# Running the last of eight experts outside the loop, and closing the trunk by token block

## What is computed

```python
h = h + moe_swiglu(hn, router_w, router_b, expert_w_gate, expert_w_up, expert_w_down)
return rms_norm(h, final_norm)      # h * rsqrt(mean(h*h) + 1e-6) * final_norm
# one expert: (silu(xb @ w_gate[e]) * (xb @ w_up[e])) @ w_down[e],  w_gate[e]: 1024 x 3584
```

## Time and profile before

| | |
|---|---|
| median of 3 runs | 1443.53 us (1442.66 to 1445.46) |
| the profiled execution | 1442.99 us, span 1441.1 us |
| TensorE matmuls busy | 1398.6 us (97%) |
| VectorE, ScalarE, GpSimd busy | 1137.7, 944.7, 20.7 us |
| granted clock, mean | 0.993 |

### The profile page before, as it was taken

The page is one execution under the profiler, slowest core; times in us unless marked ns, Lnnn a source line. Parts: engine busy times, 40 slices in busy tenths (PEclk is TensorE's granted clock), DMA queues, the critical chain, the costliest instruction groups (busy, mean ns, idle before and its releaser), DMA issues.

```text
span 1441.1 us, 17938 instructions
## 1 busy us (share of the span) xinstructions
PE 1398.6 (97%) x6483; PEld 1146.4 (80%) x6483; DVE 1137.7 (79%) x814; ACT 944.7 (66%) x773; POOL 20.7 (1%) x26
## 2 busy tenths in 40 slices
PE   6999999999979999999999999999999999999995
PEld 5888888787868887887888788788878878887884
DVE  5455666655578889888888988898898888889887
ACT  5354344445657777777777777777777777777775
POOL 0000000000120000000000000000000000000001
PEclk9999999999999999999999999999999999999998
DMA  9358775562149998998999899899989989999992
GB/s 356 106 170 225 215 207 176 175 205 88 59 135 340 371 377 304 373 369 311 367 378 355 318 370 369 315 362 365 370 307 381 363 321 372 357 353 332 368 375 85
DMA packets 192979, 423.16 MB, mean 294 GB/s; under 512 B 19184, under 2 KB 21360, under 8 KB 192944
## 3 DMA queue, kind: packets, MB, share of 16 engines
q1 hardware_dynamic: 179728, 418.15, 80.7%
q10 hardware_dynamic: 12784, 3.26, 1.6%
q0 software_dynamic: 432, 1.28, 0.3%
HBM read 421.61 MB, written 1.05 MB: 293 GB/s over the span
## 4 chain that ended last, share of the span: by engine, by line
PE 91%; DVE 3%; ACT 2%; issue 2%; POOL 0%; DMA 0%; ACTq 0%; DVEq 0%; POOLq 0%
PE bank_G L995 10%; PE bank_G L997 10%; PE bank_G L996 10%; PE bank_U L995 9%; PE bank_U L997 9%; PE bank_U L996 9%; PE bank_Y L995 8%; PE bank_Y L997 8%; PE bank_Y L996 8%; PE bank_T L1333 2%; DVE w_lo L624 1%; PE bank_G L1230 1%; PE bank_T L995 1%; PE bank_T L996 1%; PE bank_T L997 1%
## 5 line engine op out<-in xcount | busy, mean ns | idle before, releaser
L624 DVE TENSOR_TENSOR w_lo<-raw,w_hi 128x2048 fp32r<-128x2048 f32 x394 | 896.4, 2290 | 210.5 <-ACT w_hi L365 209.7
L365 ACT ACTIVATE w_hi<-raw 128x2048 fp32r<-128x2048 f32 x394 | 754.6, 1918 | 290.7 <-PE bank_U L997 93.3
L995 PE MATMUL bank_Y<-w_hi,hidT_hi 128*128 128x512 f32 x492 | 194.3, 395 | 0.0
L997 PE MATMUL bank_Y<-w_hi,hidT_lo 128*128 128x512 f32 x492 | 192.5, 391 | 0.0
L996 PE MATMUL bank_Y<-w_lo,hidT_hi 128*128 128x512 f32 x492 | 192.1, 390 | 0.0
L995 PE MATMUL bank_U<-w_hi,xg_hi 128*128 128x512 f32 x448 | 181.3, 405 | 0.5
L995 PE MATMUL bank_G<-w_hi,xg_hi 128*128 128x512 f32 x448 | 177.3, 396 | 1.4 <-DVE w_lo L624 0.5
L997 PE MATMUL bank_G<-w_hi,xg_lo 128*128 128x512 f32 x448 | 175.8, 392 | 0.0
L997 PE MATMUL bank_U<-w_hi,xg_lo 128*128 128x512 f32 x448 | 175.7, 392 | 0.0
L996 PE MATMUL bank_U<-w_lo,xg_hi 128*128 128x512 f32 x448 | 174.2, 389 | 0.0
L996 PE MATMUL bank_G<-w_lo,xg_hi 128*128 128x512 f32 x448 | 174.1, 389 | 0.0
(11 more groups left out here) (262 smaller groups left out, 1482.8 us busy)
## 6 DMA issues: line engine op xcount, KB each, us to landing
raw<-in_expert_w_gate SPq DMA_DIRECT2D x114, 1024.0 KB, 7.2
raw<-in_expert_w_up SPq DMA_DIRECT2D x113, 1024.0 KB, 7.2
raw<-in_expert_w_down SPq DMA_DIRECT2D x112, 1024.0 KB, 6.8
raw<-in_nat_w_qkv SPq DMA_DIRECT2D x12, 1024.0 KB, 5.0
raw<-in_ffn_w_gate SPq DMA_DIRECT2D x11, 1024.0 KB, 8.8
raw<-in_ffn_w_up SPq DMA_DIRECT2D x11, 1024.0 KB, 5.2
raw<-in_ffn_w_down SPq DMA_DIRECT2D x11, 1024.0 KB, 5.5
raw<-in_fourier_w_in SPq DMA_DIRECT2D x4, 1024.0 KB, 11.3
```

The costliest lines, as they stand in the source:

```text
L365: nc.scalar.activation(w_hi[w][:], raw[s][:], ACT.Copy).then_inc(hi_made, 1)
L624: nc.vector.tensor_tensor(w_lo[w][:], raw[s][:], w_hi[w][:].bitcast(f32), ALU.subtract).then_inc(lo_made, 1)
L995: nc.tensor.matmul(out_, xh, wh, start=start, stop=False)
L997: return nc.tensor.matmul(out_, xl, wh, start=False, stop=stop)
```

## The change

The loop runs over E = 0 to 6. Every engine then reads the flag and runs expert 7 once more in straight code (`expert(LAST, ...)`), with all that is for a successor left out: the three loads, the three splits, the selection, the gather with its copies, transposes and splits. The `If` follows behind it and, when taken, makes up for these. `e_scatter` counts each block and half, `e_added` each block, and `add_result` goes block by block.

The closing norm: GpSimd scales the gain row by sqrt(D) in the router stage, right behind `rstds(3)`. ScalarE squares block b as soon as its additions are done. GpSimd makes each block's factor by itself, as (sum + D eps)^-0.5. VectorE makes the output in one operation per block and half (h x factor x scaled gain), and SP stores each of the four quarters when it is made. The diff, cut:

```diff
@@ sync
+        with sp.Fori(0, LAST) as E:
+            own_loads(E)
+            next_loads(E)
         sp.wait_ge(flag_done, 1)
         over = sp.value_load(mo["flag"][0:1, 0:1], min_val=0, max_val=1)
+        own_loads(LAST)
         with sp.If(over):
...
         for b in range(NB):
-            sp.wait_ge((fin_act, fin_dve)[b], 1)
-            sp.dma_start(out[0, P * b:P * (b + 1), :], hn[:, b, :]).then_inc(s_out, 16)
+            for q in range(2):
+                sp.wait_ge(fin_done, 2 * b + q + 1)
+                cs = slice(BANK * q, BANK * (q + 1))
+                sp.dma_start(out[0, P * b:P * (b + 1), cs], hn[:, b, cs]).then_inc(s_out, 16)
@@ gpsimd
         rstds(3)
-        pool.wait_ge(moe_done, 1)
-        nc.gpsimd.tensor_tensor(hn[:, 0], h[:, 0], mo["gain"][:, 1], ALU.mult).then_inc(fin_gain, 1)
-        rstds(4)
+        nc.gpsimd.tensor_scalar(mo["gain"][:, 1], mo["gain"][:, 1], float(D) ** 0.5, None, ALU.mult).then_inc(fin_gain, 1)
+        for b in range(NB):
+            pool.wait_ge(sq_done, NB * 4 + b + 1)
+            nc.gpsimd.tensor_scalar(rstd[:, 4, b:b + 1], sumsq[:, 4, b:b + 1], D * EPS, None, ALU.add).then_inc(rstd_chain, 1)
+            pool.wait_ge(rstd_chain, 4 + 1 + b + 1)
+            nc.gpsimd.tensor_tensor(rstd[:, 4, b:b + 1], rstd[:, 4, b:b + 1], half_power[:, b:b + 1], ALU.pow).then_inc(fin_rstd, 1)
@@ scalar
             for b in range(NB):
+                if i == 4:
+                    act.wait_ge(e_added, NB * LAST + b + 1)
...
+        with act.Fori(0, LAST) as E:
+            expert(E, True)
         act.wait_ge(flag_done, 1)
         over = act.value_load(mo["flag"][0:1, 0:1], min_val=0, max_val=1)
+        expert(LAST, False)
         with act.If(over):
...
         squares(4)
-        act.wait_ge(rstd_done, 5)
-        act.wait_ge(fin_gain, 1)
-        nc.scalar.activation(hn[:, 0], hn[:, 0], ACT.Copy, scale=rstd[:, 4, 0:1]).then_inc(fin_act, 1)
@@ vector
         def add_result(E, e):
-            for q in range(2):
-                dve.wait_ge(e_scatter, 2 * E + 1 + q)
-                for b in range(NB):
+            for b in range(NB):
+                for q in range(2):
+                    dve.wait_ge(e_scatter, NB * (2 * E + q) + b + 1)
...
-            last.then_inc(e_added, 1)
+                last.then_inc(e_added, 1)
...
-        dve.wait_ge(e_added, NE)
-        dve.sem_inc(moe_done, 1)
-        dve.wait_ge(s_gain, 32)
-        link(nc.vector.tensor_tensor(hn[:, 1], h[:, 1], mo["gain"][:, 1], ALU.mult))
-        dve.wait_ge(rstd_done, 5)
-        nc.vector.tensor_scalar(hn[:, 1], hn[:, 1], rstd[:, 4, 1:2], None, ALU.mult).then_inc(fin_dve, 1)
+        dve.wait_ge(fin_gain, 1)
+        for b in range(NB):
+            dve.wait_ge(fin_rstd, b + 1)
+            for q in range(2):
+                cs = slice(BANK * q, BANK * (q + 1))
+                nc.vector.scalar_tensor_tensor(out=hn[:, b, cs], in0=h[:, b, cs], scalar=rstd[:, 4, b:b + 1],
+                                               in1=mo["gain"][:, 1, cs], op0=ALU.mult, op1=ALU.mult).then_inc(fin_done, 1)
@@ tensor
             pe.wait_ge(e_hid, E * STEPS + (STEPS - 1))
-            gather()
+            if ahead:
+                pe.wait_ge(e_sel, E + 2)
+                gather()
             down(STEPS - 2, 0)
-            transpose_tokens(E + (sweep + 2))
+            if ahead:
+                transpose_tokens(E + 2)
...
+        with pe.Fori(0, LAST) as E:
+            expert(E, True)
         pe.wait_ge(flag_done, 1)
         over = pe.value_load(mo["flag"][0:1, 0:1], min_val=0, max_val=1)
+        expert(LAST, False)
         with pe.If(over):
```

More of the change, by code:

```diff
@@ L575, in result_hi, with expert @@
                 nc.scalar.activation(mo["y_hi"][:, BANK * q:BANK * (q + 1)], Y[q][:], ACT.Copy).then_inc(e_yhi, 1)
-        def expert(E, sweep):
+        def expert(E, ahead):
             for j, (kind, c, half) in enumerate(EXPERT):
@@ L583, in expert @@
                         hidden_hi(E, c - 1)
-                if (kind, c, half) == ("up", STEPS - 1, 1):
-                    gather_copy(E + (sweep + 2))
+                if (kind, c, half) == ("up", STEPS - 1, 1) and ahead:
+                    gather_copy(E + 2)
                 if (kind, c, half) == ("down", STEPS - 2, 0):
-                    gather_hi(E + (sweep + 2))
+                    if ahead:
+                        gather_hi(E + 2)
                     hidden_hi(E, STEPS - 1)
@@ L590, in expert @@
                     result_hi(E)
-                split_hi(j + SPLIT, E)
+                if ahead or j + SPLIT < PER_EXPERT:
+                    split_hi(j + SPLIT, E)
         gather_copy(1)
@@ L595, in _ @@
         assert made[0] == N1
-        with act.Fori(*EXPERTS[0]) as E:
-            expert(E, 0)
+        with act.Fori(0, LAST) as E:
+            expert(E, True)
         act.wait_ge(flag_done, 1)
         over = act.value_load(mo["flag"][0:1, 0:1], min_val=0, max_val=1)
+        expert(LAST, False)
         with act.If(over):
[L601 to L604, removed]
+            gather_copy(NE + 1)
+            gather_hi(NE + 1)
+            for j in range(PER_EXPERT, PER_EXPERT + SPLIT):
+                split_hi(j, LAST)
+            with act.Fori(*SECOND) as E:
+                expert(E, True)
+            act.wait_ge(e_added, NB * 2 * NE)
         squares(4)
-        act.wait_ge(rstd_done, 5)
-        act.wait_ge(fin_gain, 1)
-        nc.scalar.activation(hn[:, 0], hn[:, 0], ACT.Copy, scale=rstd[:, 4, 0:1]).then_inc(fin_act, 1)
     @block.vector
@@ L920, in add_result, with expert @@
                                                           in1=part, op0=ALU.mult, op1=ALU.add)
-            last.then_inc(e_added, 1)
-        def expert(E, sweep):
+                last.then_inc(e_added, 1)
+        def expert(E, sweep, ahead):
             e = E - NE if sweep else E
@@ L927, in expert @@
                 if (kind, c, half) == ("gate", 0, 1):
-                    next_selection(E, e, sweep)
+                    next_selection(E, e, sweep, ahead)
                 elif (kind, half) == ("gate", 1):
@@ L932, in expert @@
                     hidden(E, c)
-                    if c == STEPS - 1:
-                        gather_copy(E + (sweep + 2))
+                    if c == STEPS - 1 and ahead:
+                        gather_copy(E + 2)
                 if (kind, c, half) == ("down", STEPS - 2, 0):
-                    gather_lo(E + (sweep + 2))
+                    if ahead:
+                        gather_lo(E + 2)
                     hidden_rest(E, STEPS - 1)
@@ L1389, in expert @@
             pe.wait_ge(e_selT_copy, E + 1)
-            pe.wait_ge(e_xlo, 2 * (E + (sweep + 2)))
+            if ahead:
+                pe.wait_ge(e_xlo, 2 * (E + 2))
             for q in range(2):
@@ L1396, in expert @@
                     nc.tensor.matmul(bk[:], mo["selT"][:, b], mo["y_hi"][:, cs], start=True, stop=False)
-                    last = nc.tensor.matmul(bk[:], mo["selT"][:, b], mo["y_lo"][:, cs], start=False, stop=True)
-                last.then_inc(e_scatter, 1)
+                    nc.tensor.matmul(bk[:], mo["selT"][:, b], mo["y_lo"][:, cs], start=False, stop=True).then_inc(e_scatter, 1)
         pe.wait_ge(hnr_hi, NB)
```

87 lines of the change are left out of this document (49 added, 38 removed).

## The result

| | before | after |
|---|---|---|
| median of 4 runs | 1443.22 us (1442.66 to 1445.46) | 1433.93 us (1433.89 to 1436.01) |
| profiled span | 1441.1 us | 1432.1 us |

The ratio is 0.9936, with a 95% interval of 0.9923 to 0.995: faster by 0.6%. The prediction was 1435.1, in a range of 1432.6 to 1438.7.

A forecast was written before the change was run, and what follows sets the result against it. TensorE was taken to bound the kernel nearly throughout, with 18.47 us serial from the last down product's start. Terms -2.73 - 0.13 - 6.25 + 0.1 + 0.6 = -8.4 gave span 1432.7, device time 1434.6, median 1435.1; range 1432.6 to 1438.7.

The forecast's parts named there:

- Part 1: Last expert: TensorE's gather (1.86 us) and token transposes (0.87) for a successor go, -2.73 us.
- Part 2: Seam between expert 7 and expert 8: flag read +0.15, table reload gone -0.28, together -0.13 us.
- The table load's stand: Start of the last expert: TensorE's 0.28 us wait behind ScalarE's second table load goes outside the loop.
- Part 3: Behind the last down product: earlier additions and squares, new closing norm and four smaller stores, -6.25 us.
- the exclusion: Closing norm: GpSimd's small steps and VectorE's two-SBUF-input products wait for each other; last product ends 1432.05 instead of 1431.0.
- ScalarE's jump: Behind the last product: ScalarE's jump over the skipped If delays block 0's squares by 0 to 0.6, taken as +0.1 us.
- Part 4: Router stage: GpSimd's added gain scaling, taken as 1.3 us, holds VectorE's two-input operations, +0.6 us, bounds 0 and +1.6.
- (a): Last expert: freed TensorE time is not the bound, weight splits come later, no gain there; 1437.8 us, chance 0.10.
- (b): Loop's exit: one page of code is missing, one exposed fetch of 3.49 us; 1438.6 us, chance 0.07.
- (c): Last expert starves for instructions, four exposed fetches add 14.0 us; 1449.1 us, slower than before, chance 0.03.
- (d): Tail: jump and GpSimd's exclusion eat block 0's early start (+0.5, +1.2), gain operation costs 1.6 (+1.0); 1437.8 us, chance 0.05.

The follow-up runs named there:

- e3: Changed kernel with the successor's gather, selection, copies, transposes and token splits kept in the last expert: 1436.62 us, ratio 0.9952.
- e7: Changed kernel with TensorE's read of the flag moved from the seam to behind the first gather: 1435.73 us, ratio 0.9932.
- e10: Changed kernel with the final gain scaled by ScalarE into two free PSUM banks instead of by GpSimd: 1433.49 us, ratio 0.9935.
- e4: Changed kernel with the three loads and three weight splits for a successor kept in the last expert: 1438.7 us, ratio 0.9951.
- e6: Changed kernel with GpSimd adding the gain row to itself (two inputs) where it was scaled, scaling by half the factor later: 1434.73 us, ratio 0.9927.
- e1: The kernel before, its loop over eight experts kept, with only the new closing norm and additions by block: 1441.01 us, ratio 0.9977.
- e8: Changed kernel with two experts outside the loop, which runs six times: 1435.92 us, ratio 0.9937.
- e5: Changed kernel with GpSimd's scaling of the gain row moved from the router stage to behind expert 3's additions: 1434.64 us, ratio 0.9925.
- e12: Changed kernel with 22 unread products added on TensorE where it stands in the router stage: 1435.64 us, ratio 0.9936.

## Why the prediction was right, point by point

- **Part 1** (-2.73): 2.80 by e3. Right.
- **Part 2** (-0.13): measured -0.32, the -3.12 of the last expert with its step less the 2.80 of the gather. The step grew by 0.12 (0.15 predicted), but that is partly covered, as in e7: at the first product of up, after is 0.07 later behind the scatter than before. The table load's stand is gone as predicted, and it was worth 0.39 and not 0.28: 0.28 ahead of the product at 1312.45, and 0.11 in the step behind it (0.34 to the next start, 0.23 in after).
- **Part 3** (-6.25): -7.11, the term that was mis-sized most. The last product of VectorE ends 8.89 us behind the last down product, 9.42 predicted; the rest of the way 2.47, where I had 2.80. The first difference (0.53) is nearly all the exclusion: I took 1.05; measured are 0.28 and 0.35 on the two steps, and by e10 0.57 at VectorE's last product, 0.39 of them in the tail. As predicted, the small step slips in between VectorE's two products and the power waits for them; but it ends 0.43 behind the pair's end (1428.18 and 1427.75), where I had given it its whole 0.72, the duration of 128x2; alone it takes 0.58. The second (0.33) is the way from that product to the end of the span, where the stores landed in 2.0 to 2.4.
- **ScalarE's jump** (+0.1): 0.05 us, and the squares start 0.03 behind their addition. TensorE's 3.49 was no measure for it. The Trainium skill (Runtime: NRT & Kernel Launch, Instruction fetch mechanics) has a taken branch out of the buffered window wait for a fetch. The trace fits that on TensorE (3.56) and shows no such wait on ScalarE (0.05); whether ScalarE's jump leaves its window no run here shows.
- **Part 4** (+0.6): +0.12 in after, 0 in e7, up to 0.83 in e4. Two errors cancelled in part: the scaling takes 2.79 and not 1.3, more than the 2.3 that I gave as its upper bound, but a one-input operation doesn't hold every operation of VectorE to its end, as I had assumed. With two inputs it does: 0.96 in e6. The Trainium skill (SBUF — State Buffer, Who interferes with whom) has a VectorE instruction with two SBUF inputs and a GpSimd one that reads SBUF exclude each other for the whole instruction; by e6, e4 and e1 the trace agrees where GpSimd's long operation has two inputs (1.13 instead of 0.17) and where a small step of GpSimd comes second (2.34 instead of 0.23). In after it doesn't: two-input operations of VectorE pass at 0.17 beside the one-input scaling of 2.79 that came first. There the measurement decides.
- **Not in the sum:** +0.30 in "tokens", which goes with the clock's later return (the first four transposes take 1.05 us instead of 0.75), +0.15 in the seven experts, and +0.66 of arrival, there ahead of the router stage.
- **The rivals:** (a) by e3, (b) and (c) by e8 and by TensorE's busy 119.18 of 119.18, (d) by the squares and the router column. All four fall. Against the prediction's span of 1432.7 the errors are -0.86 (part 3), -0.48 (part 4), -0.10 (jump), -0.07 (part 1) and -0.19 (part 2), then +0.15, +0.30 and +0.66: -0.59, and the span came out 0.6 lower. So the mechanism is right in parts 1 to 3 and wrong for the jump of ScalarE and for the one-input scaling of part 4, and the closeness is in part luck: the terms alone are off by -1.7, and 1.1 of it was given back by things that no term held. The device time is 1.2 under the 1435.1 because the 0.54 from the profiled run to the median, which I added from before, didn't come again: after's profiled run (1433.90) lies at its median.

## What to carry to other kernels

Price a stretch behind the last product by what still stands in it for a successor: two unneeded splits cost as much here (3.55 us, e4) as the new norm gained by itself (3.50, e1). An edit's gain is better read between two stations of the trace than from the span, since two runs differ by 2 us ahead of any changed line. An operand moved to PSUM freed the other engine, and the two copies for it (1.18 us) lay in idle time of ScalarE. A step that is made shorter gains nothing where the next wait takes it back, as at the seam in e7.

## What the runs showed of the hardware

- GpSimd and VectorE: with two SBUF inputs on VectorE and a GpSimd operation beside them, whoever starts second mostly waits. 0.23 us becomes 2.34 beside a w_lo of 2.28; two operations of 2.3 us asked for at once take 4.3 to 4.6 for the second. A one-input GpSimd operation of 2.79 us takes 6.97 among VectorE's splits, and in the router stage holds some of VectorE's small operations (`eq` for 0.12 in four traces, `idx` for 0.36 to 0.83 in three) and not others, in e7 none. What tells them apart stays open.
- TensorE's granted clock falls to 0.50 behind the router stage's stand of some 4 us, but also behind one of 1.9 to 2.1 us near 411 (e1, e4, e5, e7, e8) and within one of 1.23 us in e12. Behind the router stage it comes back between 424 and 432, by run and kernel. The gather's products step at 0.43 us under it, and each product of the first expert caught by it costs 0.20 more.
- Code executed for the first time costs TensorE nothing visible in a stretch without a jump, with one expert (five packets fetched) or with two (nine).
